# The turn of the experts' hidden rows moved from TensorE to VectorE and ScalarE in a one-core decoder step

## What is computed

```python
hb = jax.nn.silu(jnp.einsum('nd,edf->nef', xb, ex_w1)) * jnp.einsum('nd,edf->nef', xb, ex_w3)
return jnp.einsum('nef,efd->nd', hb * gb[..., None], ex_w2)
```

## Time and profile before

| | |
|---|---|
| median of 3 runs | 1023.09 us (1022.70 to 1023.42) |
| the profiled execution | 1023.74 us |
| its span | 1022.0 us |
| TensorE busy | 975.8 us, 95% |
| VectorE busy | 452.9 us, 44% |
| GpSimd busy | 352.1 us, 34% |
| ScalarE busy | 146.4 us, 14% |
| mean DMA rate over the span | 291 GB/s |

### The profile page before, as it was taken

The page is one execution under the profiler, slowest core; times in us unless marked ns, Lnnn a source line. Parts: engine busy times, 40 slices in busy tenths (PEclk is TensorE's granted clock), DMA queues, the critical chain, the costliest instruction groups (busy, mean ns, idle before and its releaser), DMA issues.

```text
span 1022.0 us, 16640 instructions
## 1 busy us (share of the span) xinstructions
PE 975.8 (95%) x6109; PEld 436.6 (43%) x6109; DVE 452.9 (44%) x1319; ACT 146.4 (14%) x358; POOL 352.1 (34%) x439
## 2 busy tenths in 40 slices
PE   7999999999999899999999999899997899999996
PEld 5777555655545333333333333233332233333442
DVE  3411221344568634444443434444434443442885
ACT  4000023301022000010001010001000001112332
POOL 6000331300043644442543434444433344440232
PEclk9999999999999999999999999999998999999999
DMA  8033224222076989999999999999999999988932
GB/s 282 2 94 104 83 74 119 101 63 73 21 247 262 387 327 377 406 412 400 412 411 411 408 409 416 411 408 407 413 403 393 383 413 400 409 329 337 421 134 83
DMA packets 76118, 297.54 MB, mean 291 GB/s; under 512 B 15622, under 2 KB 26062, under 8 KB 49149
## 3 DMA queue, kind: packets, MB, share of 16 engines
q1 hardware_dynamic: 60133, 258.68, 64.8%
q0 software_dynamic: 15904, 37.79, 9.6%
HBM read 276.56 MB, written 31.50 MB: 301 GB/s over the span
## 4 chain that ended last, share of the span: by engine, by line
PE 73%; DMA 12%; DVE 5%; issue 4%; POOL 3%; DVEq 1%; another core or an unknown queue 1%; SPq 0%; ACT 0%; POOLq 0%; ACTq 0%
PE bank L2331 26%; PE bank L1982 22%; PE bank L2326 8%; PE bank L2429 5%; DMA arena<-xs_dram,slot 5%; DMA arena<-in_ex_w 3%; DMA ring<-in_ex_w 3%; PE bank L1988 2%; POOL arena L988 2%; PE bank L2381 1%; PE bank L2159 1%; PE bank L2086 1%; PE bank L2076 1%; PE bank L2123 1%; DMA x<-in_x_prompt 1%
## 5 line engine op out<-in xcount | busy, mean ns | idle before, releaser
L2331 PE MATMUL bank<-arena 128*32 128x512 f32 x1440 | 272.5, 596 | 2.7 <-DMA ring<-in_ex_w 1.9
L988 POOL DMA_INDIRECT arena<-xs_dram,slot x192 | 210.5, 1096 | 73.2 <-issue 62.8
L2331 PE MATMUL bank<-ring,arena 128*32 128x512 f32 x864 | 214.9, 604 | 3.4 <-DMA arena<-in_ex_w 2.2
L1004 POOL DMA_INDIRECT y_dram<-arena,outrow x46 | 47.1, 1023 | 267.5 <-DVE slot L1773 218.8
L2331 PE MATMUL bank<-xT,arena 128*32 128x512 f32 x576 | 115.3, 607 | 5.2 <-DMA ring<-in_ex_w 5.2
L2331 PEld LDWEIGHTS bank<-arena 128*32 128x32 f32 x1440 | 72.1, 110 | 99.2 <-issue 93.3
L1982 PE MATMUL bank<-xT,ring 128*128 128x288 f32 x384 | 93.4, 406 | 0.0
L1787 DVE STREAM_TRANSPOSE arena<-arena 128x1024 f32<-128x1024 f32 x48 | 59.7, 1244 | 73.1 <-DMA arena<-xs_dram,slot 68.7
L2331 PE MATMUL bank<-mixpj,arena 128*32 128x512 f32 x384 | 84.7, 594 | 0.0
L1982 PEld LDWEIGHTS bank<-xT,ring 128*128 128x128 f32 x384 | 72.9, 190 | 20.5 <-DMA ring<-in_w_in 0.5
L1852 DVE SCALAR_TENSOR_TENSOR arena<-bank,gate,arena 128x256 f32<-128x256 f32 x46 | 22.3, 484 | 128.3 <-ACT arena L1198 119.9
(11 more groups left out here) (422 smaller groups left out, 1269.0 us busy)
## 6 DMA issues: line engine op xcount, KB each, us to landing
arena<-in_ex_w SPq DMA_DIRECT2D x78, 1024.0 KB
ring<-in_ex_w SPq DMA_DIRECT2D x50, 1024.0 KB
xT<-in_ex_w SPq DMA_DIRECT2D x28, 1024.0 KB
mixpj<-in_ex_w SPq DMA_DIRECT2D x24, 1024.0 KB
arena<-y_dram SPq DMA_DIRECT2D x18, 1024.0 KB, 10.7
wide<-in_ex_w SPq DMA_DIRECT2D x12, 1024.0 KB
ring<-in_w_in SPq DMA_DIRECT2D x5, 2048.0 KB, 9.3
ring<-in_w_out SPq DMA_DIRECT2D x2, 2048.0 KB, 8.8
```

What stands on the lines that cost most here:

```text
L988: pool.indirect_dma_start(xg[b][:, 256 * a:256 * a + 256], None, xs_quarter, bass.IndirectOffsetOnAxis(slot[k][:, a:a + 1], 0), bounds_che ...
L1004: pool.indirect_dma_start(y_dram, bass.IndirectOffsetOnAxis(outrow[b][:, 0:1], 0), og[b], None, bounds_check=K * T - 1, oob_is_err=False). ...
L2331: ins = pe.matmul(b[t, :], lhs[:, t], rhs(home(own if lane < 3 else common)), start=start, stop=stop)
```

## The change

The two transposes on TensorE and the copy of `bank[4]` go. VectorE turns `hh` in blocks of 32x32 into `hz`, which is the memory of `hu`. A block transpose leaves every block in its own quarter of the partitions (its quadrant), so ScalarE then moves them: sixteen copies of 32 partitions by 2x32 elements each, one for every pair of source and target quadrant. The semaphore `s_pht` becomes `s_z`. The wait for `hh` that stood ahead of the transposes on TensorE becomes a wait ahead of mm1 of the next step, since that overwrites `bank[2]`.

```diff
+        hz = hu.rearrange("p (c k t) -> p c k t", c=2, t=LANE)
...
 (ScalarE, step j)
                     if not first:
                         out(base, half, j)
-                    act.wait_ge(s_pht, base + (j + 1))
-                    act.copy(hT, bank[4][:, 0:2 * P].rearrange("p (c t) -> p c t", t=P)).then_inc(s_hT, 1)
+                    act.wait_ge(s_z, base + (j + 1))
+                    for a in range(4):
+                        for k in range(4):
+                            ins = act.copy(hT[LANE * k:LANE * k + LANE, :, LANE * a:LANE * a + LANE],
+                                           hz[LANE * a:LANE * a + LANE, :, k, :])
+                    ins.then_inc(s_hT, 1)
...
 (VectorE, step j)
                     dve.scalar_tensor_tensor(out=hh, in0=bank[2][:, FF:2 * FF], scalar=gate[depth(j)][:, 0:1],
                                              in1=hs, op0=ALU.mult, op1=ALU.mult).then_inc(s_h, 1)
+                    if j:
+                        dve.wait_ge(s_hT, base + j)
+                    dve.wait_ge(s_h, base + (j + 1))
+                    dve.transpose(hz, hh.rearrange("p (k i c) -> p c k i", k=4, c=2)).then_inc(s_z, 1)
...
 (TensorE, step j)
+                    if j:
+                        pe.wait_ge(s_h, base + j)
                     pe.wait_ge(s_xgT, base + (j + 1))
...
                     if j:
                         mm2(base, r, j - 1)
-                    pe.wait_ge(s_h, base + (j + 1))
-                    for c in range(2):
-                        ins = pe.transpose(bank[4][:, P * c:P * c + P], hh[:, c:FF:2], ident[:, :])
-                    ins.then_inc(s_pht, 1)
```

More of the change, by code:

```diff
@@ L448, in decoder_step @@
         (s_cols, s_inq, s_onehot, s_index, s_picked, s_gate, s_h, s_xgT, s_out1, s_silu, s_hT, s_out0,
-         s_psel, s_mm1, s_pht, s_mm2) = (sem(n) for n in (
+         s_psel, s_mm1, s_z, s_mm2) = (sem(n) for n in (
              "s_cols", "s_inq", "s_onehot", "s_index", "s_picked", "s_gate", "s_h", "s_xgT", "s_out1", "s_silu",
-             "s_hT", "s_out0", "s_psel", "s_mm1", "s_pht", "s_mm2"))
+             "s_hT", "s_out0", "s_psel", "s_mm1", "s_z", "s_mm2"))
         s_y8 = [[sem(f"s_y8_{b}{q}") for q in range(4)] for b in range(2)]
```

## The result

| | before | after |
|---|---|---|
| median of the runs | 1022.89 us (6 runs) | 1029.07 us (6 runs, 1027.29 to 1030.54) |
| ratio | | 1.0049, interval 1.0030 to 1.0068 |
| profiled execution, its span | 1023.74, 1022.0 us | 1027.58, 1025.8 us |

A forecast was written before the change was run, and what follows sets the result against it. Full DMA queues, with the gather-to-pick chain as tight, were taken as the bound. Profiled 1023.74 us - 2.0 (idle DMA time) + 1.6 (end copies) + 1.6 (clock) = 1024.9 us, so 1024.3 us for the runs, range 1018.5 to 1029.0 us.

The forecast's parts named there:

- What bounds the kernel: Expert loop: full DMA queues near 410 GB/s bind, and the 20.2 us chain from `out` to the pick is as tight.
- What the removal gives TensorE: From mm2 to mm1: 0.52 us saved in each of 45 places in the loop, 23 us of TensorE's time, the ceiling.
- What of that reaches the end: Loop: loads issued sooner use a fifth to a third of the idle DMA time, 2 us gained, between 0 and 9.7.
- VectorE: Its new transpose in each step takes 0.31 to 0.4 us, hidden in more than 3 us of idle time.
- ScalarE in the loop: The sixteen copies take 2.5 us, 1.9 to 4.1, and cost nothing inside the loop.
- ScalarE at the end: After the last step the copies delay the last mm2 by 2.1 us; 1.6 us are left after slack.
- The clock there: At the last mm2: a wait of about 3.2 us brings half clock for about 3.4 us, losing 1.6 us.
- The slack behind the end: Behind the last mm2, VectorE's late copy gives back 0.5 us of the 2.1 us delay.
- Rival 3: Slower: longer weight waits, each followed by half clock, 1027.8 us; or end copies without overlap, 1028.0 us. Together chance 0.30.
- Rival 1: Whole loop: DMA queues have room and TensorE is the bound, so about 1003 us; chance 0.03.
- rival 2: Loop: more than half or all idle DMA time used, 5.5 to 9.7 us, so 1020.8 to 1015 us; chance 0.15.

The follow-up runs named there:

- e10: The changed kernel with a quarter of nearly every w3 transfer and only the first of four gathers per step: 970.7 us, 514.9 us to mm2 of step 44.
- e9: The kernel before with a quarter of nearly every w3 transfer and only the first of four gathers per step: 986.8 us, 534.9 us to mm2 of step 44.
- a0: The changed kernel run and profiled again, unaltered: ratio 1.0042 to the kernel before.
- e2: The kernel before, but in step 45 only the rows are turned by VectorE and the sixteen copies: ratio 1.0019 to the kernel before.
- e1: The changed kernel, but in step 45 TensorE turns the rows and ScalarE makes one copy, as before: ratio 1.0023 to the kernel before.
- e3: The changed kernel with one ScalarE copy of 128x256 in place of the sixteen, leaving out the moves between quadrants: ratio 1.0026 to the kernel before.
- e7: The changed kernel, but in the last step the sixteen copies stand ahead of the out copy and write to another buffer: ratio 1.0041 to the kernel before.
- e8: The changed kernel with nine unread matmuls keeping TensorE busy in its wait ahead of the last mm2: ratio 1.0057 to the kernel before.

## Why the prediction was right or wrong

The forecast was no change, on the slow side, 1024.3 us in a range of 1018.5 to 1029.0 us. The kernel is slower by 0.5%: 1028 us by the ratio, near the top of the range, while the median of the runs, 1029.07 us, lies just over it. The direction and the bound were right for the reasons given. The size is in part luck, since terms were off with opposite signs and half of the loss isn't in the forecast at all. By the steps:

- **What bounds the kernel**: right, and shown. Full queues and the chain of gather, turn, one-hot tiles and pick each hide TensorE's saving by itself; it takes both reliefs to see it (the table), which rest on two runs and one profile each.
- **What the removal gives TensorE**, 0.52 us in each of 45 places: right (0.43 us from group to group across the change of product; 20.0 us in e10 against e9).
- **What of that reaches the end**, the term of - 2.0 us: wrong in size, it was + 0.3 us in the profile and 0.3 to 1.7 us in the six profiles with the new steps. The step that failed is that a load issued sooner into an idle gap brings the loop's end forward. In the first profile the three windows shown moved 28, 9 and 5 GB/s more and the last loads were issued 6.2 us sooner, and the mm1 behind them started 0.6 us later all the same; in the second (`a0`) neither the gain nor the lead is there. Why the stream ended no earlier is open: the trace has no landing for those loads.
- **VectorE**: right that it is hidden. The transpose takes 0.45 us, not 0.31 to 0.4. Its source is read with a stride of two elements, but no run tests whether that is why.
- **ScalarE in the loop**: right. `hT` was ready well before the next mm1 ended.
- **ScalarE at the end**, + 1.6 us: mis-sized. The copies took 4.07 us, the upper bound of 4.1, not 2.5: they don't overlap. I took the spacing from copies out of PSUM that start at the same partition. The trace of before has a nearer pair, two copies out of different halves of a bank on ScalarE's timeline, 0.58 us long and 0.59 us apart:

```profile
924.71 0.58 ACT L1176 COPY mixpj<-bank 64x512 f32<-64x512 f32 x1 [1.19 <-PE bank L1989]
925.30 0.58 ACT L1177 COPY mixpj<-bank 64x512 f32<-64x512 f32 x1
```

- **The clock there**, + 1.6 us: right in kind. It cost 2.1 us in the first profile (5.78 against 3.65 us), where the fall lasted 6.8 us, and 1.4 us in `a0`, where it lasted 3.4 us behind the same wait of 4.9 us.
- **The slack behind the end**: 0.5 us was reckoned, and the tail gave back 2.7 to 3.7 us, in the main by the scatter's shorter landing. So the end as a whole costs 1.9 us (e2), where the forecast had 3.2: two errors of opposite sign.
- **Rival 3** came nearest, by its time and by its second case, copies without overlap. Of its first case, waits for weights followed by half clock, the signs are mixed: inside the loop the changed kernel's profiles have nine and eight spans of 3.4 us at half clock and the one before has three, but e1, with the new loop, and e2, with the old one, have five each (all of them have one more at 343 to 346 us, at the loop's start). The price that I put on such a wait, 1.2 us, was too high, since the loop to mm2 of step 44 lost only 0.3 us. Rival 1 is refuted (1003 us asked for), and so is rival 2 (1015 to 1020.8 us): even where the first window moved 364 GB/s in place of 336, nothing was gained. Its chance had rested on the same step that failed.

Still open: the 2.3 to 2.6 us that e1 and e3 lose. Their loops are 0.5 to 1.0 us longer in the profiles, and e1's tail is 2.7 us longer with 1.7 us of it from half clock in the gate products; one profile of each is too few to say that this is the rule, and their runs scatter over 7 us.

No version here that does the whole work beats the kernel before.

## What to carry to other kernels

When two resources are each near full, work taken from a third shows up as waiting for them, and lifting one of the two shows nothing: test both, one at a time and together, before concluding that the saving was not there. A resource's idle share in a window is no estimate of what can be gained: it moves from one profile of a kernel to the next (364 and 333 GB/s here), and what counts is whether the transfer that the end waits for would land sooner. And a cost that the loop hides is bare in its last round, so price a longer latency there first, from rows of the same shape and the same partitions.

## What the runs showed of the hardware

- Copies on ScalarE of 32 partitions by 64 elements, each with another source or target quadrant than the one ahead, are 0.244 us long and 0.255 us apart within every row of sixteen, in both orders (736 copies in each profile). The pair of copies out of PSUM that start at the same partition overlaps by 0.09 us.
- The same wait of TensorE, 4.9 us ahead of the last mm2, came with a stretch at half clock of 6.8 us in one profile of the changed kernel and of 3.4 us in the other. A gap that is removed at one place can open at another: the waits ahead of the gate products grew from 0.70 us before to 2.07 to 2.91 us in e1, e3, e7 and e8, and the clock fell there.
- The last scatter lands in 3.8 us when issued at 931 us and in 6.8 us at 925 us, for the same bytes. In the second case a 2 MB load was under way beside it and landed 0.5 us behind it.
